# A hybrid decoder step: state copies on the sync queue, sums of the down weights a product ahead, samples without an operand of their own

## The chip, the cores and the metric

The kernel runs on one core of a Trainium2 chip. Its time is device microseconds of one execution; of three runs the median was 1857.97 us (1844.95 to 1858.78). The rows below come from one further, profiled execution, which took 1857.11 us, with a span of 1855.3 us between its first and last recorded instruction.

## The reference, cut to what matters

One decoder layer is computed in float32 for two groups of requests that share the weights: one prompt of 1024 tokens (positions 0 to 1023) and 64 sample tokens (8 requests with 8 tokens each, behind 2048 past tokens).

- RMSNorm, then one input projection (1024 to 1952 columns) that feeds two kinds of attention, a multi-head latent one and a dilated sliding-window one, 8 heads each.
- The heads' outputs pass an output projection (1024 x 1024) and are added to the input: h.
- RMSNorm, then a gated MLP: `g = xn @ w_gate`, `u = xn @ w_up` (1024 x 2816), a causal depthwise convolution of width 3 over g, `silu(gc) * u`, and `@ w_down` (2816 x 1024), added to h. A last RMSNorm gives y.
- Outputs besides y: keys, values and latents of the new tokens, the last rows of g, and **the window state of the samples**: for k and v each, `concatenate([state, new])[-2048:]` along 2048 rows of 512 numbers for 8 requests. 2040 of the 2048 rows are a plain copy from the input, shifted by 8: about 67 MB for k and v together.

## The kernel before, in words

Three phases follow each other, each a block in which the five engines run their own instruction lists, tied by semaphores: `project`, `attention` (the longest) and `output_and_mlp`. Every float32 product is made of three float32r products: a factor is split in a high part (a cast, ACT) and a low part (a subtraction, on DVE or POOL), and high x high, high x low, low x high are added up in PSUM.

**The state copy** (`move`, L192 to L198) is done in 20 chunks of 102 rows. A chunk is four DMAs from DRAM to DRAM, k and v, even and odd rows, 816 KB each. All 80 are issued from ACT's queue: 5 chunks in `project` at the end of a token tile's work (L595), 3 in the output projection (L2724), 12 in the MLP loop after `gate_first(f)` (L2767), f in `moving`. All other DMAs of these phases are issued by SP, in the order in which they are written.

**`project`.** 9 token tiles of 128 rows. For tile t TensorE (PE) makes four groups of projection products (L816), and in between turns the normalised latent `cn` (L828). `cn` comes from PE's first group by way of ACT (squares, L523 and L525), POOL (root) and DVE (L680). SP's list for a tile is `stores(t)`.

**`output_and_mlp`.** The output projection also goes by token tiles (L3102), each followed by a turning of the normalised tile (L3114) whose result ACT and DVE copy and split (`turned`). SP stores h (`store_h`) and loads the next operand (`load_o`).

The MLP is one level of Strassen's scheme in Winograd's form: 7 products of half size for 8. The loop goes over f, 22 blocks of 128 hidden columns (FC = 22). For each f there are 7 products of 24 matmuls (L3122). The weights of block f + 2 are loaded (`load_raw`) as soon as block f's are split; ACT makes high parts, POOL sums and low parts; DVE gathers the results. `gated(f)` makes `us` (the product with silu) and `diff`, the difference of its two token halves (L2897), which lies in the first half of `u3`. `store_a(f)` writes both to scratch `s_a`. `fourth(f)`, which overwrites `u3`, therefore waits for the landing of `diff`'s store (L2907), `up_second(f)` for that of `us` (L2914).

**The down projection** comes last: again 7 products, in the order p1, p2, p5, p3, p6, p7, p4, and each of them in 11 steps (HF = 11) over the hidden dimension, 77 steps n in all. A step is 12 matmuls (L3214): 4 token tiles x 3 float32r terms. The operand from the activations is a piece of `s_a` that SP loads into a ring of 6 places (`load_piece`); for p5, p3 and p6 it is a sum of two pieces, which DVE adds (L2951). The weights `w_down` (11 loads of 1 MB, `load_w`) stay in SBUF; p5, p6, p7 and p4 need differences of their blocks, which POOL makes in place, each right before the step that uses it (L2550). Per step ACT casts both operands (L2671, L2682), DVE makes the low part of the activations (L2840) and POOL that of the weights (L2552). There are 4 operand slots, so these engines can be at most about three steps ahead of PE. When a product is done, DVE adds its four banks to `acc` (L2971); the first add waits for h, which SP has loaded back (`h_in`).

The samples' rows have no halves to combine. In p1, p2, p5 and p3 a step has two more matmuls (L3205) with the samples' activations. For p5 they need a weight block that the product itself doesn't use; it is cast and split into an operand of its own, `extra` (`high_x` L2684, `low_x` L2955).

## Time and profile before

| | us |
|---|---|
| median of 3 runs | 1857.97 |
| lowest, highest | 1844.95, 1858.78 |
| the profiled execution | 1857.11 |
| its span | 1855.3 |

| engine | busy us | share |
|---|---|---|
| PE | 1659.6 | 89% |
| DVE | 1060.3 | 57% |
| ACT | 783.3 | 42% |
| POOL | 961.0 | 52% |

The project phase ends about 290 us into the span, the attention phase at about 902 us, the output projection's first MLP product starts at 1028 us, the MLP loop's second block at 1068 us, and the down projection at 1549 us. In the rows, a line number such as L198 is that of the kernel; "idle before <- releaser" in brackets is how long an engine stood still before an instruction and what ended that; ACTq and SPq are the sequencers of ACT and SP, on which the issue of a DMA takes time.

### The profile page before, as it was taken

What the parts mean: (1) busy time and instruction counts of PE and PEld (TensorE: products, weight loads), DVE (VectorE), ACT (ScalarE), POOL (GpSimd) and SP (SyncE); (2) the same over time, 40 slices, a digit from 0 to 9 for tenths busy, and PEclk for the clock granted to TensorE, in tenths of its full rate; (3) what the DMA queues carried; (4) which work ended last, traced back from release to release, by engine and by line L of the source; (5) the groups of instructions that cost most, each with busy time, mean ns of one, the idle gap of its engine ahead of it and who ended that gap; (6) DMA issues with size and microseconds to landing.
All of it is one profiled execution on the core that took longest, in us unless ns stands there. A gap on an engine that the chain in (4) does not pass through costs nothing.

```text
span 1855.3 us, 29370 instructions
## 1 busy us (share of the span) xinstructions
PE 1659.6 (89%) x10253; PEld 1474.2 (79%) x10253; DVE 1060.3 (57%) x1896; ACT 783.3 (42%) x1639; POOL 961.0 (52%) x825
## 2 busy tenths in 40 slices
PE   7987996999997899999999699899998998979876
PEld 6776775888886788888777699899998997767655
DVE  6523334767775677667443855565554544477664
ACT  5212113666776667666422433333332323333333
POOL 1000001655753668677401877676776762364886
PEclk9998997999999999999999799999999999999999
DMA  8255455233214565655656145546554569634431
GB/s 278 99 170 180 161 175 143 54 101 95 53 52 119 158 175 161 182 160 180 219 152 225 62 126 158 178 159 207 158 156 159 163 207 350 203 108 148 136 115 61
DMA packets 214956, 285.09 MB, mean 154 GB/s; under 512 B 35639, under 2 KB 134584, under 8 KB 209656
## 3 DMA queue, kind: packets, MB, share of 16 engines
q1 hardware_dynamic: 181534, 216.42, 38.2%
q10 hardware_dynamic: 33280, 66.85, 11.0%
q8 instruction: 81, 1.33, 0.3%
q14 instruction: 61, 0.50, 0.1%
HBM read 235.66 MB, written 114.41 MB: 189 GB/s over the span
## 4 chain that ended last, share of the span: by engine, by line
PE 17%; POOL 7%; DMA 6%; DVE 6%; ACTq 6%; issue 4%; ACT 4%; SPq 1%; POOLq 0%; DVEq 0%
ACTq L198 6%; PE r_ps L3122 5%; PE z_ps L3122 3%; POOL d_w L2550 3%; PE q_ps L3122 3%; DMA scratch_s_a<-acc 2%; DMA o_work<-scratch_s_o 2%; POOL lead L2552 1%; POOL u_op L2552 1%; PE q_ps L3102 1%; DMA d_w<-in_w_down 1%; PE v_ps L3122 1%; PE r_ps L3214 1%; PE z_ps L3214 1%; DVE d_ring L2951 1%
## 5 line engine op out<-in xcount | busy, mean ns | idle before, releaser
L1111 POOL TENSOR_SCALAR a_pr<-a_pr,a_rden 128x256 f32<-128x256 f32 (+7 forms) x128 | 94.1, 746 | 192.6 <-DVE a_rden L1211 187.9
L2466 POOL TENSOR_TENSOR lead<-acc,lead 128x512 fp32r<-128x512 f32 x110 | 155.8, 1433 | 38.0 <-ACT lead L2613 37.8
L2840 DVE TENSOR_TENSOR lead<-d_ring,lead 128x512 fp32r<-128x512 f32 x73 | 70.9, 973 | 94.1 <-ACT lead L2671 93.8
L816 PE MATMUL zp<-win_h,xT_h 128*128 128x512 f32 (+1 forms) x288 | 116.4, 404 | 3.3 <-DVE acc L667 3.3
L816 PE MATMUL zp<-win_l,xT_h 128*128 128x512 f32 (+1 forms) x288 | 114.5, 397 | 0.0
L2466 POOL TENSOR_TENSOR u_op<-acc,u_op 128x512 fp32r<-128x512 f32 x44 | 56.6, 1289 | 107.7 <-ACT u_op L2613 98.8
L1152 ACT ACTIVATE a_pr<-a_pr,a_nm 128x256 f32<-128x256 f32 (+7 forms) x128 | 98.5, 772 | 20.0 <-DVE a_nm L1205 19.3
L816 PE MATMUL zp<-win_h,xT_l 128*128 128x512 f32 (+1 forms) x256 | 101.8, 398 | 0.0
L467 POOL TENSOR_TENSOR st<-st 128x2 f32<-128x2 f32 x9 | 1.7, 193 | 189.5 <-ACT cn L525 189.5
L1285 PE MATMUL a_o<-a_ph,a_vh 128*128 128x256 f32 x288 | 87.7, 305 | 13.5 <-DVE a_pl L1215 13.3
L2613 ACT CAST lead<-acc 128x512 fp32r<-128x512 f32 x105 | 62.7, 618 | 74.1 <-PE z_ps L3122 31.1
L2671 ACT CAST lead<-d_ring 128x512 fp32r<-128x512 f32 x73 | 45.1, 618 | 108.4 <-DVE d_ring L2951 52.1
L2552 POOL TENSOR_TENSOR u_op<-d_w,u_op 128x512 fp32r<-128x512 f32 x39 | 53.2, 1366 | 70.0 <-ACT u_op L2682 70.0
L1285 PE MATMUL a_o<-a_pl,a_vh 128*128 128x256 f32 x288 | 82.7, 287 | 0.0
L1285 PE MATMUL a_o<-a_ph,a_vl 128*128 128x256 f32 x288 | 82.5, 286 | 0.0
L3122 PE MATMUL z_ps<-u_s4h,lead 128*128 128x272 f32 x352 | 68.2, 309 | 15.6 <-DVE u_us L2915 15.6
L2552 POOL TENSOR_TENSOR lead<-d_w,lead 128x512 fp32r<-128x512 f32 x38 | 52.2, 1374 | 56.6 <-ACT lead L2682 56.6
L3122 PE MATMUL r_ps<-u_a12h,u_op 128*128 128x272 f32 x352 | 64.1, 295 | 14.0 <-ACT acc L2630 14.0
L1953 ACT CAST w_kth<-l_bank 128x384 fp32r<-128x384 f32 (+2 forms) x96 | 49.5, 517 | 63.5 <-PE l_bank L2051 41.5
L2613 ACT CAST u_op<-acc 128x512 fp32r<-128x512 f32 x42 | 26.0, 621 | 116.3 <-issue 81.3
L1974 DVE TENSOR_TENSOR w_ktl<-l_bank,w_kth 128x384 fp32r<-128x384 f32 (+2 forms) x96 | 57.7, 601 | 27.6 <-ACT w_kth L1953 27.0
L2550 POOL TENSOR_TENSOR d_w<-d_w 128x512 f32<-128x512 f32 x44 | 72.5, 1648 | 0.0
(438 smaller groups left out, 5551.2 us busy)
## 6 DMA issues: line engine op xcount, KB each, us to landing
out_s_win_k<-in_state_win_k ACTq DMA_DIRECT2D x40, 816.0 KB
out_s_win_v<-in_state_win_v ACTq DMA_DIRECT2D x40, 816.0 KB
d_ring<-scratch_s_a SPq DMA_DIRECT2D x106, 256.0 KB, 2.7
acc<-in_state_win_k SPq DMA_DIRECT2D x16, 768.0 KB, 5.6
acc<-in_state_win_v SPq DMA_DIRECT2D x16, 768.0 KB, 5.5
scratch_s_a<-u_us SPq DMA_DIRECT2D x22, 544.0 KB, 6.5
acc<-in_w_gate SPq DMA_DIRECT2D x23, 512.0 KB, 6.5
acc<-in_w_up SPq DMA_DIRECT2D x22, 512.0 KB, 7.4
```

What stands on the lines that cost most here:

```text
L198: eng.dma_start(b[s], a[s]).then_inc(io["moved"], 16)
L816: last = nc.tensor.matmul(z[:, 0:n], a, b, start=(k == 0 and i == 0), stop=(k == KC - 1 and i == len(terms) - 1))
L1111: nc.gpsimd.tensor_scalar(p, p, self.rden[:, k % 2, h:h + 1], 1.0, ALU.mult, ALU.mult)\
L1152: nc.scalar.activation(p, p, ACT.Exp, bias=self.nm[:, k % 2, last, h:h + 1], scale=-1.0, accum_out=self.den[:, k % 2, h:h + 1]).then_inc(S ...
L1285: last = nc.tensor.matmul(self.o_bank[:], x[:, kb, :], y[:, kb], start=(kb == 0 and i == 0), stop=(kb == s and i == 2))
L1974: sub = lambda out, a, b: nc.vector.tensor_tensor(out, a, b.bitcast(F32), ALU.subtract)
L2466: nc.gpsimd.tensor_tensor(op[n][:, 1, :], src, op[n][:, 0, :].bitcast(F32), ALU.subtract).then_inc(S["lo"], 1)
L2550: nc.gpsimd.tensor_tensor(w, a, c, ALU.subtract).then_inc(S["t_sum"], 1)
L2552: nc.gpsimd.tensor_tensor(ob[n % SLOTS][:, 1, :], w, ob[n % SLOTS][:, 0, :].bitcast(F32), ALU.subtract)\
L2613: copy(op[n][:, 0, :], src).then_inc(S["hi"], 1)
L2840: less = lambda out, a, b: tt(out, a, b.bitcast(F32), ALU.subtract)
L3122: last = nc.tensor.matmul(region[:, c * 512:c * 512 + PIECE], op[w][:, a, k * P:(k + 1) * P], X[x][b][:, k, c * PIECE:(c + 1) * PIECE], st ...
```

## The change

1. **State copies.** `move` becomes `move_rows(eng, io, chunk, part)`, one DMA of the four. All 80 are issued by SP: in `project` four in each of the `stores(t)` for t = 2 to 6, one behind the store of the latents, one behind that of the keys, one behind the rotation load and one at the end; in the output projection one behind `load_o` for t < 8; in the MLP loop 2 or 3 at the end of SP's list for each f < 20. ACT issues none.
2. **`diff`.** It gets a place of its own in two halves of 256 columns, made by two subtractions and stored by two DMAs. `fourth(f)` no longer waits for its store; `gated(f)` waits for that of block f - 1.
3. **Order of SP's loads before the down projection.** Pieces 4 to 11 come after six of the eleven weight loads instead of after ten; the other five weight loads are spread over what follows; the ring has 10 places instead of 6.
4. **Sums of the down weights.** p5's differences are made by POOL in p2's steps, p6's by POOL in p3's; p7's and p4's by DVE, two steps ahead.
5. **Samples.** `extra` goes. The samples' sums are taken out of the bank after p1 (into columns 512 to 1023), after p2 (0 to 511, p1 and p2 together) and after p3 (512 to 1023, p5 and p3), so that p5 can use the operand of the product itself. In a product's first step they come last instead of first.

```diff
-def move(eng, io, first, rows):
-
-    for src, dst in (("state_win_k", "s_win_k"), ("state_win_v", "s_win_v")):
...
+def move_rows(eng, io, chunk, part):
+
+    src, dst = (("state_win_k", "s_win_k"), ("state_win_v", "s_win_v"))[part // 2]
+    a = io[src][:, bass.ds(chunk * CHUNK + DEC_T, CHUNK), :].rearrange("b (r s) c -> s b r c", s=2)
+    b = io[dst][:, bass.ds(chunk * CHUNK, CHUNK), :].rearrange("b (r s) c -> s b r c", s=2)
+    eng.dma_start(b[part % 2], a[part % 2]).then_inc(io["moved"], 16)
...
                 store_c(t)
+                move_rows(sp, io, t.n - 2, 0)
                 store_dq(t)
                 store_dk(t)
+                move_rows(sp, io, t.n - 2, 1)
                 store_q(t)
                 if not ends(t):
                     turns_in(t)
+                move_rows(sp, io, t.n - 2, 2)
                 store_dv(t)
                 store_kv(t)
+                move_rows(sp, io, t.n - 2, 3)
...
-                if not isinstance(t.n, int) or t.n == 6:
-                    move(act, io, (t.n - 2) * CHUNK, CHUNK)
...
+        diff0 = ctx.enter_context(nc.sbuf_tensor("u_diff0", [P, 256], F32, side="right"))
...
-        diff = u3[:, 0:512]
+        diff_at = sx_at + DEC_B * (DEC_T + CONV_W - 1)
+        diff = (diff0[:], flat[:, diff_at:diff_at + 256])
...
-                sp.dma_start(s_a[f, :, TOK:A_COLS], diff).then_inc(S["d_st"], 16)
+                for i in range(2):
+                    sp.dma_start(s_a[f, :, TOK + 256 * i:TOK + 256 * i + 256], diff[i]).then_inc(S["d_st"], 16)
...
-                if m >= 10:
-                    sp.wait_ge(S["a_lo"], step_of[m - 6] + 1)
+                if m >= 14:
+                    sp.wait_ge(S["a_lo"], step_of[m - 10] + 1)
...
+                if t < PT:
+                    move_rows(sp, io, 5 + t // 4, t % 4)
...
                 if f:
                     store_a(f - 1)
-            for q, free in ((0, "p1"), (1, "p1"), (2, "p6"), (3, "p6"), (4, "p2"), (5, "p2"), (6, "p7"), (7, "p7"),
-                            (8, "p5"), (9, "p5"), (10, "p4")):
-                sp.wait_ge(S["product"], MADE[free, FC - 1])
-                if q == 10:
-                    for m in range(4, 8):
-                        load_piece(m)
+                for u in range(28 + 52 * f // 20, 28 + 52 * (f + 1) // 20 if f < 20 else 0):
+                    move_rows(sp, io, u // 4, u % 4)
+            made = lambda n: sp.wait_ge(S["product"], MADE[n, FC - 1])
+            for q, n in ((0, "p1"), (1, "p1"), (2, "p6"), (3, "p6"), (4, "p2"), (5, "p2")):
+                made(n)
                 load_w(q)
+            made("p4")
+            for m in range(4, 8):
+                load_piece(m)
+            made("p3")
+            for m in range(8, 12):
+                load_piece(m)
             store_a(FC - 1)
+            load_w(6)
             sp.wait_ge(S["a_st"], 16 * FC)
...
+            load_w(7)
+            sp.wait_ge(S["lo"], 7 * FC)
+            load_h(2, 4)
+            sp.wait_ge(S["a_lo"], 4)
+            load_h(0, 2)
+            load_w(8)
             sp.wait_ge(S["last_ev"], 6)
             sp.dma_start(io["p_ffn_conv"], last_rows[0:CONV_W - 1, :]).then_inc(S["rows_out"], 16)
             sp.dma_start(io["s_ffn_conv"], last_rows[CONV_W - 1:LASTS, :]).then_inc(S["rows_out"], 16)
...
+            load_piece(14)
+            load_w(9)
             sp.wait_ge(S["rows_out"], 32)
             load_h(4, PT)
+            load_piece(15)
+            load_w(10)
+            sp.dma_start(g_last, io["g_final"].partition_broadcast(P)).then_inc(S["h_in"], 16)
...
-                if p in ("p5", "p6", "p7", "p4"):
+                if p == "p2":
                     pool.wait_ge(*w_in(j))
+                    nc.gpsimd.tensor_tensor(w_half(j, 0), w_half(j, 1), w_half(j, 0), ALU.subtract).then_inc(S["t_sum"], 1)
+                elif p == "p3":
                     pool.wait_ge(*w_in(j + HF))
...
+                    pool.wait_ge(S["t_sum"], j + 1)
+                    nc.gpsimd.tensor_tensor(w_half(j, 0), w_half(j + HF, 1), w_half(j, 0), ALU.subtract).then_inc(S["t_sum"], 1)
                 pool.wait_ge(S["b_hi"], n + 1)
...
-            def high_x(j):
...
-                if t % 2 == 0:
-                    move(act, io, (t // 2 + 4) * CHUNK, CHUNK)
...
-                if f in moving:
-                    move(act, io, (8 + moving.index(f)) * CHUNK, CHUNK)
...
-                if n == 5:
+                if n == 4:
                     lasts_out(0, 3)
...
-                tt(diff, us[:, 0:512], us[:, 512:SEQ], ALU.subtract).then_inc(S["act"], 1)
+                if f:
+                    dve.wait_ge(S["d_st"], 32 * f)
+                for i in range(2):
+                    c = 256 * i
+                    last = tt(diff[i], us[:, c:c + 256], us[:, 512 + c:768 + c], ALU.subtract)
+                    last.then_inc(S["act"] if i else S["sink"], 1)
...
                 dve.wait_ge(S["product"], MADE["p7", f])
-                if f:
-                    dve.wait_ge(S["d_st"], 16 * f)
...
-            def low_x(j):
...
+            def third(j):
+                dve.wait_ge(S["t_sum"], HF + j + 1)
+                a = w_half(j, 1)
+                tt(a, w_half(j + HF, 1), a, ALU.subtract).then_inc(S["d_sum"], 1)
+
+            def fourth_sum(j):
+                dve.wait_ge(S["t_sum"], HF + j + 1)
+                dve.wait_ge(S["b_lo"], HF + j + 1)
+                a = w_half(j + HF, 0)
+                tt(a, a, w_half(j, 0), ALU.subtract).then_inc(S["d_sum"], 1)
...
+                if n + 2 < len(STEPS):
+                    p, j = STEPS[n + 2]
+                    if p == "p7":
+                        third(j)
+                    elif p == "p4":
+                        fourth_sum(j)
                 low_a(n)
...
-                if n == 13:
+                if n == 12:
                     dve.wait_ge(S["h_in"], 80)
+                if n in (12, 23, 45):
+                    sample_add(n // HF - 1)
...
                     if k == 3:
+                        if j == 0 and p in ("p1", "p2", "p5", "p3"):
+                            if p in ("p2", "p5"):
+                                pe.wait_ge(S["s_done"], 1 if p == "p2" else 2)
+                            last = sample(p, j, b)
                         last.then_inc(S["step"], 1)
```

## Rows read from the trace of the kernel before

**Rows 1.** The page's top, and its chain of waits by line (shares of the span).
```profile
span 1855.3 us, 29370 instructions
...
ACTq L198 6%; PE r_ps L3122 5%; PE z_ps L3122 3%; POOL d_w L2550 3%; PE q_ps L3122 3%; DMA scratch_s_a<-acc 2%; DMA o_work<-scratch_s_o 2%; POOL lead L2552 1%; POOL u_op L2552 1%; PE q_ps L3102 1%; DMA d_w<-in_w_down 1%; PE v_ps L3122 1%; PE r_ps L3214 1%; PE z_ps L3214 1%; DVE d_ring L2951 1%
```
**Rows 2.** The page's DMA queue of ACT: packets, MB, share of 16 engines' span.
```profile
q10 hardware_dynamic: 33280, 66.85, 11.0%
```
**Rows 3.** Line L198, the copies' issue on ACT: ns min/median/max, first and last start.
```profile
L198 ACTq DMA_DIRECT2D out_s_win_v<-in_state_win_v x40: 679/3592/10944, 100.6 to 1515.1; - x40
```
**Rows 4.** ACT in order of time, one tile of project: start us, us, [idle before <-releaser].
```profile
134.29 10.13 ACTq L198 DMA_DIRECT2D out_s_win_v<-in_state_win_v  x2
144.88 1.07 ACT L512 CAST xT_h<-xp 128x512 fp32r<-128x512 f32 x2 [11.57 <-issue]
```
**Rows 5.** PE's line L828, 98 to 250 us: busy, mean ns | idle before <-releaser.
```profile
L828 PE MATMUL cp<-ident_sb,cn 128*128 128x128 f32 x15 | 4.5, 439 | 24.0 <-DVE cn L680 24.0
```
**Rows 6.** Windows in project: length, busy PE, PEld, DVE, ACT, POOL; PEclk, DMA share, GB/s.
```profile
82.70:245.50 162.80, 138.83 (x626) 116.35 (x624) 47.02 (x127) 28.55 (x70) 8.21 (x20) 0.93 0.50 164
245.50:272.50 27.00, 26.99 (x118) 22.57 (x119) 8.94 (x30) 4.85 (x12) 0.89 (x2) 0.94 0.56 175
```
**Rows 7.** PE in order of time, output projection: the three long stops.
```profile
968.32 0.74 PE L3102 MATMUL z_ps<-lead,o_th 128*128 128x512 f32 x2 [2.79 <-DVE o_tl L2840]
...
997.27 1.54 PE L3114 MATMUL v_ps<-ident_sb,o_work 128*128 128x128 f32 x6 [4.04 <-DVE o_work L2869]
...
1026.57 1.75 PE L3114 MATMUL v_ps<-ident_sb,o_work 128*128 128x128 f32 x7 [6.08 <-DVE o_work L2869]
```
**Rows 8.** Windows of the MLP loop: blocks 1 to 21, block 7, block 15.
```profile
1067.80:1549.10 481.30, 455.45 (x3529) 450.72 (x3529) 267.80 (x276) 161.93 (x336) 326.93 (x227) 0.98 0.54 174
1204.96:1226.11 21.15, 21.15 (x171) 21.14 (x170) 12.65 (x13) 7.56 (x16) 14.50 (x11) 1.00 0.52 169
1381.68:1413.54 31.86, 23.74 (x170) 23.19 (x169) 15.97 (x17) 9.74 (x23) 20.81 (x15) 0.89 0.63 206
```
**Rows 9.** Who waited for whom: us in total, times, longest us.
```profile
DVE acc L2908 <- DMA scratch_s_a<-acc: 52.9, 10, 11.0
```
**Rows 10.** SP's queue in order of time, two blocks of the MLP: start us, us.
```profile
1211.58 0.34 SPq L2343 DMA_DIRECT2D scratch_s_a<-u_us  x1
...
1276.59 3.24 SPq L2343 DMA_DIRECT2D scratch_s_a<-u_us  x1
```
**Rows 11.** The page's DMA issues: KB each, median us from issue to landing.
```profile
scratch_s_a<-u_us SPq DMA_DIRECT2D x22, 544.0 KB, 6.5
```
**Rows 12.** Windows of the down projection: p1 with p2, then p5, p3, p6, p7, p4.
```profile
1549.10:1638.70 89.60, 78.25 (x332) 62.11 (x330) 43.05 (x54) 30.11 (x56) 38.03 (x26) 0.94 0.68 236
1638.70:1687.40 48.70, 39.14 (x154) 29.33 (x155) 36.73 (x38) 17.78 (x32) 25.96 (x18) 0.97 0.36 110
1687.40:1723.00 35.60, 35.60 (x156) 28.97 (x155) 25.41 (x30) 12.87 (x22) 18.41 (x14) 1.00 0.52 161
1723.00:1757.90 34.90, 31.61 (x133) 24.32 (x132) 24.16 (x23) 11.57 (x19) 28.31 (x20) 1.00 0.48 143
1757.90:1803.30 45.40, 33.97 (x132) 25.36 (x132) 30.38 (x29) 17.76 (x32) 36.97 (x33) 0.96 0.38 116
1803.30:1845.10 41.80, 33.06 (x130) 25.17 (x131) 18.66 (x24) 13.92 (x29) 32.07 (x24) 0.96 0.10 26
```
**Rows 13.** The chain of waits in order of time, before DVE's first adds: start us, us.
```profile
1589.99 8.35 DMA acc<-scratch_s_h
```
**Rows 14.** Groups from 1560 us on: POOL's sums and low parts; busy us, mean ns.
```profile
L2550 POOL TENSOR_TENSOR d_w<-d_w 128x512 f32<-128x512 f32 x44 | 72.5, 1648 | 0.0
...
L2552 POOL TENSOR_TENSOR lead<-d_w,lead 128x512 fp32r<-128x512 f32 x36 | 49.1, 1367 | 52.9 <-ACT lead L2682 52.9
```
**Rows 15.** DVE in order of time, two steps of p3.
```profile
1698.80 1.79 DVE L2951 TENSOR_TENSOR d_ring<-d_ring 128x512 f32<-128x512 f32 x1
1701.33 0.69 DVE L2840 TENSOR_TENSOR lead<-d_ring,lead 128x512 fp32r<-128x512 f32 x1 [0.74 <-ACT lead L2671]
```

More of the change, by code:

```diff
@@ L3133, in lasts_turn, with sample @@
                     last.then_inc(S["last_ps"], 1)
+            def sample(p, j, b):
+                rows_s = (sh0 if p in ("p1", "p5") else sh1)[:, j, :]
+                for h in range(2):
+                    last = nc.tensor.matmul(s_bank, rows_s, b[:, h, :], start=p in ("p1", "p5") and j == 0 and h == 0,
+                                            stop=p != "p5" and j == HF - 1 and h == 1, skip_group_check=p == "p2")
+                if p != "p5" and j == HF - 1:
+                    last.then_inc(S["s_ps"], 1)
+                return last
             products(0)
```

97 lines of the change are left out of this document (24 added, 73 removed).

## The prediction

> **What bounds the kernel now.** I start at the page's top and its chain of waits by line. PE is busy for 89% of the span, yet the line with the largest share of the chain is not PE's: it is L198, the issue of the state copies on ACT's queue, with 6% of 1855.3 us, about 110 us [rows 1]. A chain share is an upper bound, not a gain. So the second look goes to each stage: what does PE stand still for, and what ended that wait?
>
> The copies take little DMA time: ACT's queue holds 11.0% of the engines for 80 copies, 204 us / 80 = 2.55 us each [rows 2]. But the issue of one took up to 10.9 us, median 3.6 us for v, which comes third and fourth [rows 3]. In project the last two of a chunk hold ACT for 10.1 us, and its next cast has stood idle for 11.6 us, with nothing but issue before it [rows 4]. That is the whole mechanism: an issuer can run a few copies ahead of the DMA engines, then it stands, and all of ACT's compute stands behind it.
>
> Who waits for ACT there? PE at the turning of the latent: 24.0 us in five tiles [rows 5]. Five tiles with copies last 162.8 / 5 = 32.6 us each; the next one, without, lasts 27.0 us with PE busy throughout [rows 6]. The same three times in the output projection: 2.79, 4.04 and 6.08 us [rows 7]. In the MLP loop a block without disturbance lasts 21.15 us, PE 100% busy; block 15, with ACT held in it and in block 14, lasts 31.86 us, at a granted clock of 0.89, that is partly at 1.2 instead of 2.4 GHz after PE had stood; the 21 blocks last 481.3 us [rows 8]. Part of that stop is not ACT's: `fourth` waits ten times, 52.9 us in all, for the store of `diff` [rows 9].
>
> The down projection is a different case. p3 lasts 35.6 us with PE busy throughout, 3.24 us per step of 14 matmuls; 12 of them are 3.24 x 12/14 = 2.77 us, 30.5 us for 11 steps. p5 lasts 48.7, p7 45.4 and p4 41.8 us [rows 12]. In p7 POOL is busy 36.97 us, in p4 32.07: sum (1.65 us), ACT's cast, low part (1.37 us), one behind the other in every step [rows 14]. Here POOL is the bound. In p5 DVE is, with three instructions per step and 36.73 us busy [rows 12].
>
> **The change part by part.** Gains and losses in us of the profiled execution (1857.1, within 1 of the median of the runs).
>
> *Copies in project.* Five tiles go from 32.6 to 27.0 us: 5 x 5.6 = 28 [rows 6]. ACT's list gets shorter; SP's gets four issues per tile, 4 x 2.55 = 10.2 us of DMA in a tile whose DMA share is 0.50 of 32.6 = 16.3 us, those copies included [rows 2, 6]. 16.3 of 27.0 us fits. Next late would be a store or the next x behind a copy, about 2.6 us; I take 26, bounds 12 and 29.
>
> *Copies in the output projection.* Stops of 12.9 us [rows 7], and clock behind them; eight copies instead of twelve. The first stop came from a late `load_o`, and now a copy follows every `load_o` on the same queue, so part comes back. Bounds 4 and 17; I take 12, because two of the three stops hang on ACT.
>
> *Copies and `diff` in the MLP loop.* 481.3 - 21 x 21.15 = 37 us above the undisturbed block [rows 8]. ACT's hold goes for certain; the wait of `fourth` goes with the new place of `diff` [rows 9]. New: 2.6 copies per block on SP, 6.6 us, behind the weight loads and the stores of their block. DMA is busy 0.54 x 22.9 = 12.4 us per block, copies included [rows 8], so it drains before the next loads. SP's next duty is a block away. The store of `us` already waits 3.24 us for its issue when it follows the weight loads closely, and 0.34 us when it doesn't [rows 10]: SP feels the same limit, but with slack. That store lands 6.5 us after its issue [rows 11]; its user, `up_second`, comes behind the fifth product of the block, and the row with 0.34 us is of block 7, which starts at 1204.96: 1204.96 + 5 x 3.02 (a seventh of 21.15) = 1220.1, 8.5 us after 1211.6 [rows 8, 10]. 2 us of slack. The two subtractions of 256 for one of 512 cost DVE between 0 and 0.7 us (another such instruction, rows 15), covered while DVE is busy 12.65 of 21.15 us [rows 8]; the extra store is one SP issue of 0.34 us. I take 34, bounds 15 and 38.
>
> *Down projection, p1 and p2*: 89.6 us, against 71.2 at 3.24 per step [rows 12]. Earlier pieces take away a stop of PE in p1. But DVE's first adds need all of h, the last of which lands at 1589.99 + 8.35 = 1598.3 [rows 13], 49 us into a stage where the same bytes must still come, and now five weight loads stand among them. Most of p1's gain is therefore waited away again at p2's first step; the sample's wait at p5's first step, now last in it, goes. I take 81, bounds 75 and 92.
>
> *p5*: no `extra` (11 casts, 11 DVE splits), no POOL sum. 35.6 plus 1.4 for bank waits at its start: 37, bounds 35.6 and 42.
> *p3*: POOL gets the sums of p6: two instructions, 3.0 us of 3.24 [rows 14], but no longer with a cast between them. 36.5, bounds 35.6 and 41.
> *p6*: POOL is relieved, and DVE's own cycle of sum, ACT's cast and low part shows: 2.53 us between the starts of rows 15 and 0.6 until the next sum, 3.15 per step against PE's 2.77. The three steps of lead pay for most of the 4 us. 33, bounds 30.5 and 37.
> *p7*: POOL is relieved (36.97 us busy before), DVE gets 11 more sums to its 30.38 us [rows 12]: 11 x 0.7 = 7.5, less the waits for POOL contained in those 30. 37, bounds 31 and 45.
> *p4*: DVE 18.66 + 7 = 26 of 30.5 us. 32.5, bounds 30.5 and 41.8.
> Sum 81 + 37 + 36.5 + 33 + 37 + 32.5 = 257 for 296: 39.
>
> In all 26 + 12 + 34 + 39 = 111: 1857.1 - 111 = **1746 us**.
>
> One row bears on the two engines that share p3, p7 and p4: a DVE sum of two SBUF tiles takes 1.79 us when it starts beside POOL's low part, where the next DVE instruction takes 0.69 [rows 15]. The Trainium skill, page "SBUF — State Buffer", section "Who interferes with whom", has the rule: a DVE instruction with two SBUF inputs and a POOL instruction that reads SBUF exclude each other, for the whole instruction. By that rule the trace agrees, and moving sums from POOL to DVE frees less than it seems.
>
> **Rivals.**
> *DVE and POOL block each other (0.15).* For it: 1.79 against 0.69 us [rows 15], and 11 more such DVE instructions each in p7 and p4. Then p7 and p4 stay at 45.4 and 41.8 and p3 rises to 41 (two POOL instructions of 1.37 and one DVE sum squeezed in, 3.7 per step): 8.4 + 9.3 + 4.5 = 22 less, 1768. Against it: in all three the cast is no longer between two POOL instructions, and both engines can work ahead.
> *Half of the copies' gain comes back (0.12).* SP is held as ACT was [rows 10], and loads and stores behind copies come 2.6 us late each: half of 26 + 12 + 34 is lost, 1782. For it: the 2 us of slack above; against it: DMA share 0.54.
> *Slower (0.02).* Copies of the block before stand in front of `us`'s store in each block: 2.6 x 2.55 = 6.6 us, 20 blocks of 27.8 us, 133 above the floor for 37 now, nothing gained in project and the output projection: 1857 + 96 - 39 = 1914. It decides from the point where DMA work per block passes 21 us; the rows show 12.4. The Trainium skill, page "DMA: Bandwidth & Descriptors", section "Queues, rings and completion order", speaks for this one: DMA engines take turns between queues, but work one queue's descriptors off in order, so a copy on SP's own queue stands wholly in front of what SP issues next. No row here shows that order, as no copy shared SP's queue.
> *No gain (0.03).* ACT's holds were covered and another wait replaces each, as in the chain after a stop; only p5 improves, by 12: 1845. Against it: tile and blocks without copies in rows 6 and 8.
>
> **How the numbers follow.** The forecast has 0.68. For the range: all upper bounds together give 29 + 17 + 38 + 58 = 142, which won't all come; three quarters of the way from 111 is 24, to 1722. Upwards it takes in both middling rivals: 1788. About 1% of the time, 18 us, is what a measurement of this kernel can tell from no change. Faster by over 1%: 0.68 + 0.15 + 0.12 = 0.95, same 0.03, slower 0.02.
>
> **What would show it.** ACT has no DMA issue; no stop of PE at L828 in tiles 2 to 6, tiles of 27 us; every MLP block at 21.2; no wait of L2908's kind for a store; SP's copy issues of up to some us, with nobody waiting. PE's wait at p2's first step for adds after h. p5 at 37, p7 and p4 without POOL as releaser. The forecast is wrong if MLP blocks show DVE waiting for the store of `us`, or if p7 and p4 keep their length with DVE as releaser.

## The result and the profile after

The changed kernel takes 1758.3 us (median of four runs, 1754.4 to 1762.8), the kernel before 1851.5 us (1840.5 to 1858.8): ratio 0.950, 95% interval 0.944 to 0.957. The forecast was 1746 us, range 1722 to 1788. Below, the profiled execution of 1761.3 us, span 1759.5 us.

The windows of the changed kernel that answer to [rows 6, 8, 12]: project's five tiles with copies, the 21 MLP blocks, one of these blocks, then p1 with p2, p5, p3, p6, p7, p4. Columns as there.

```profile
82.80:214.59 131.79, 129.90 (x627) 110.29 (x625) 48.19 (x130) 28.60 (x70) 8.41 (x20) 1.00 0.66 211
1023.25:1489.60 466.35, 447.10 (x3529) 442.76 (x3529) 292.99 (x298) 164.28 (x339) 321.13 (x227) 1.00 0.59 184
1222.54:1244.84 22.30, 21.30 (x171) 21.08 (x170) 13.96 (x14) 7.71 (x17) 15.65 (x11) 1.00 0.63 191
1489.60:1575.90 86.30, 75.68 (x329) 61.01 (x328) 37.87 (x53) 27.94 (x50) 41.66 (x32) 0.92 0.72 250
1575.90:1611.30 35.40, 35.40 (x155) 28.94 (x154) 27.23 (x28) 12.56 (x22) 18.11 (x14) 1.00 0.49 150
1611.30:1647.40 36.10, 36.10 (x158) 29.48 (x157) 28.20 (x28) 11.80 (x21) 30.15 (x20) 1.00 0.49 153
1647.40:1682.90 35.50, 32.71 (x134) 24.13 (x134) 28.49 (x30) 14.16 (x26) 15.83 (x12) 1.00 0.51 155
1682.90:1718.40 35.50, 31.75 (x133) 24.24 (x131) 35.50 (x43) 17.96 (x32) 28.61 (x21) 1.00 0.42 131
1718.40:1748.50 30.10, 29.98 (x130) 24.35 (x130) 24.51 (x29) 12.11 (x25) 23.06 (x15) 1.00 0.09 29
```

The span laid side by side, in us; the cuts are PE's stop ahead of attention, its stop ahead of the output projection, and the first product of MLP block 1:

| stretch | before | after | change | forecast |
|---|---|---|---|---|
| start to attention | 279.05 | 246.55 | -32.5 | -26 |
| attention | 621.4 | 623.2 | +1.8 | 0 |
| output projection and block 0 | 167.4 | 153.5 | -13.8 | -12 |
| MLP blocks 1 to 21 | 481.3 | 466.4 | **-15.0** | **-34** |
| p1 and p2 | 89.6 | 86.3 | -3.3 | -8.6 |
| p5, p3 | 84.3 | 71.5 | -12.8 | -10.8 |
| p6, p7, p4 | 122.1 | 101.1 | -21.0 | -19.6 |
| rest | 10.2 | 11.0 | +0.8 | 0 |
| sum | 1855.3 | 1759.5 | -95.8 | -111 |

The parts of the change were not all taken apart: the down projection's 37 us come from the changed load order, sums and samples together, and the windows show where that gain falls, not which of the three makes it.

One line is far off: the MLP loop. Its clock is 1.00 now and no block is held up by a copy; yet each lasts about 22.3 us instead of 21.15. Two lines of PE's list of waits (total, times, longest); the first heads it and is new:

```profile
PE q_ps L3128 <- DVE acc L2898: 23.1, 20, 4.0
...
PE r_ps L3219 <- DVE acc L2972: 10.6, 1, 10.6
```

L2898 is the add of `second`. It reads PE's bank q_ps, which p7, the fourth product of a block in PE's order, then overwrites. What DVE does ahead of it, from its timeline in one block:

```profile
1228.59 1.29 DVE L2886 TENSOR_TENSOR u_us<-u_us,u_gc 128x1088 f32<-128x1088 f32 x1 [0.55 <-ACT u_gc L2660]
1229.91 1.40 DVE L2892 TENSOR_TENSOR u_diff<-u_us 128x256 f32<-128x256 f32 x1
1231.24 1.51 DVE L2892 TENSOR_TENSOR acc<-u_us 128x256 f32<-128x256 f32 x1
1232.68 0.71 DVE L2898 TENSOR_TENSOR acc<-q_ps,acc 128x544 f32<-128x544 f32 x1
```

and POOL and PE at the same time:

```profile
1228.65 2.38 POOL L2490 TENSOR_TENSOR acc<-acc 128x512 f32<-128x512 f32 x1
1230.99 1.47 POOL L2492 TENSOR_TENSOR acc<-acc 128x512 f32<-128x512 f32 x1
...
1233.44 0.39 PE L3128 MATMUL q_ps<-u_s3h,lead 128*128 128x272 f32 x1 [1.00 <-DVE acc L2898]
```

Two subtractions of 256 columns take 2.9 us; the one of 512 in the kernel before took 1.67. DVE's first ends at 1231.31, just behind POOL's end at 1231.03; its second at 1232.75, behind POOL's end at 1232.46. DVE's instructions end when POOL's do, so cutting one in two bought a second turn of waiting. The same trace holds the counter-example. After the last block POOL does nothing from 1492.07 to 1497.02, and there the same two subtractions take 0.43 and 0.42 us (DVE, then POOL):

```profile
1494.82 0.43 DVE L2892 TENSOR_TENSOR u_diff<-u_us 128x256 f32<-128x256 f32 x1
1495.16 0.42 DVE L2892 TENSOR_TENSOR acc<-u_us 128x256 f32<-128x256 f32 x1
...
1497.02 1.28 POOL L2554 TENSOR_TENSOR u_op<-d_w,u_op 128x512 fp32r<-128x512 f32 x1 [4.96 <-ACT u_op L2686]
```

20 blocks x 1.15 us are 23 us; the time missed the forecast by 12.

The copies of v themselves, now on SP's queue (count, shortest/median/longest issue in ns; those of k are alike), against up to 10.9 us in [rows 3]:

```profile
L197 SPq DMA_DIRECT2D out_s_win_v<-in_state_win_v x40: 674/702/2412, 95.0 to 1436.1; - x40
```

I had expected copy issues "of up to some us" on SP. The longest is 2.5 us and the median 0.7. What follows a copy on SP's queue does feel it: in project the issue of the next x takes 3.2 to 5.2 us in three tiles (below). The short issues made me doubt the reason that I had given for the copies' gain, and half of the experiments are about it.

### The profile page after: what moved, and what is told of

The parts are those of the page before. It is cut to its first block, busy times and chain, and to the rows that moved or that the text cites. A ratio compares the mean times of both kernels' runs of the same rounds, so it can differ in the third digit from the quotient of the medians.

```text
span 1759.5 us, 29359 instructions
## 1 busy us (share of the span) xinstructions
PE 1629.3 (93%) x10253; PEld 1456.8 (83%) x10253; DVE 1092.2 (62%) x1931; ACT 778.7 (44%) x1628; POOL 930.6 (53%) x803
## 4 chain that ended last, share of the span: by engine, by line
PE 21%; DVE 15%; issue 6%; ACT 3%; DMA 3%; POOL 2%; SPq 1%; ACTq 0%; POOLq 0%; DVEq 0%
PE q_ps L3128 4%; PE z_ps L3128 4%; PE v_ps L3128 4%; PE z_ps L3108 3%; DVE d_ring L2945 2%; PE q_ps L3108 2%; DVE acc L2892 2%; PE z_ps L3219 2%; DVE u_gc L2937 1%; DVE u_us L2886 1%; DVE u_gc L2934 1%; ACT u_gc L2660 1%; DVE acc L2972 1%; ACT lead L2673 1%; PE v_ps L3219 1%
## 5 line engine op out<-in xcount | busy, mean ns | idle before, releaser
L2476 POOL TENSOR_TENSOR lead<-acc,lead 128x512 fp32r<-128x512 f32 x110 | 143.7, 1316 | 126.4 <-ACT lead L2615 126.4
L1153 ACT ACTIVATE a_pr<-a_pr,a_nm 128x256 f32<-128x256 f32 (+7 forms) x128 | 98.6, 772 | 22.1 <-DVE a_nm L1206 21.3
L2831 DVE TENSOR_TENSOR lead<-d_ring,lead 128x512 fp32r<-128x512 f32 x73 | 59.0, 808 | 55.0 <-ACT lead L2673 55.0
L2554 POOL TENSOR_TENSOR lead<-d_w,lead 128x512 fp32r<-128x512 f32 x38 | 61.4, 1618 | 54.9 <-ACT lead L2686 54.4
L3128 PE MATMUL q_ps<-u_s3h,lead 128*128 128x272 f32 x352 | 65.3, 298 | 23.2 <-DVE acc L2898 23.1
L2554 POOL TENSOR_TENSOR u_op<-d_w,u_op 128x512 fp32r<-128x512 f32 x39 | 58.2, 1495 | 53.6 <-ACT u_op L2686 53.0
L3128 PEld LDWEIGHTS q_ps<-u_s3h,lead 128*128 128x128 f32 x352 | 51.7, 192 | 27.8 <-DVE acc L2898 27.8
L1286 PEld LDWEIGHTS a_o<-a_ph,a_vh 128*128 128x128 f32 x288 | 56.6, 196 | 18.3 <-issue 15.9
L3128 PE MATMUL z_ps<-u_s4h,lead 128*128 128x272 f32 x352 | 64.0, 295 | 3.1 <-DVE u_us L2909 3.1
L3128 PE MATMUL v_ps<-u_a22h,lead 128*128 128x272 f32 x352 | 64.0, 295 | 1.5 <-issue 1.5
L817 PEld LDWEIGHTS zp<-win_h,xT_h 128*128 128x128 f32 x288 | 54.8, 190 | 12.4 <-DVE acc L668 3.5
```

Source lines behind the costliest of these rows:

```text
L817: last = nc.tensor.matmul(z[:, 0:n], a, b, start=(k == 0 and i == 0), stop=(k == KC - 1 and i == len(terms) - 1))
L1153: nc.scalar.activation(p, p, ACT.Exp, bias=self.nm[:, k % 2, last, h:h + 1], scale=-1.0, accum_out=self.den[:, k % 2, h:h + 1]).then_inc(S ...
L1286: last = nc.tensor.matmul(self.o_bank[:], x[:, kb, :], y[:, kb], start=(kb == 0 and i == 0), stop=(kb == s and i == 2))
L2476: nc.gpsimd.tensor_tensor(op[n][:, 1, :], src, op[n][:, 0, :].bitcast(F32), ALU.subtract).then_inc(S["lo"], 1)
L2554: nc.gpsimd.tensor_tensor(ob[n % SLOTS][:, 1, :], w, ob[n % SLOTS][:, 0, :].bitcast(F32), ALU.subtract)\
L2831: less = lambda out, a, b: tt(out, a, b.bitcast(F32), ALU.subtract)
```

## The experiments

All times are medians; ratios are to the kernel before, with 95% intervals. Each edit is made to the changed kernel unless it says otherwise.

### The copies' part alone: before_sp

The kernel before with nothing changed but `move`: ACT's calls go, and SP gets the calls of `move_rows` at the changed kernel's places.

```diff
-                if f in moving:
-                    move(act, io, (8 + moving.index(f)) * CHUNK, CHUNK)
...
+                for u in range(28 + 52 * f // 20, 28 + 52 * (f + 1) // 20 if f < 20 else 0):
+                    move_rows(sp, io, u // 4, u % 4)
```

> The kernel before, with one part of the change alone: the state copies leave ACT's queue and go on the sync engine's queue, one quarter of a chunk at a time at the changed kernel's places (project, output projection, MLP loop). Difference, down projection and load order as before. Theory A (ACT's hold is the whole cost of the copies and is not paid elsewhere): project -32 us, output projection -14 (both as measured between the two kernels), MLP loop at 21.0 to 21.3 us per block where it was 22.9 on average, -33 or more, the down projection as before; in all 1852 - 80 = 1770 to 1778. Theory B (the difference's new place is needed for the MLP loop's gain, the add's wait for its store stays): MLP blocks 22 or more, 1790 or more. Theory C (only half of the gain, copies in front of stores on the same queue): 1810.

Measured 1772.7 us, 0.958 (0.953 to 0.964): 79 us from the copies. Nineteen MLP blocks and the PE time in them:

```profile
1041.34:1443.34 402.00, 402.00 (x3195) 401.84 (x3193) 243.11 (x248) 146.94 (x304) 298.26 (x210) 1.00 0.62 191
```

402.0 / 19 = 21.16 us per block, PE never idle, with `diff` still in `u3` and its 512 columns in one. So theory A, and the loop's whole gain, about 37 us, was to be had from the copies alone. My terms for the copies (26 + 12 + 34 = 72) were nearly right in sum; the change gave 22 us of them back by another part.

### Engine or group: act_parts, sp_fours, act_fours

Two properties of the copies changed together, the issuing engine and the size of the group. These three kernels fill in the square. "Quarters" means one copy at a time in project and in the output projection, and two or three in a row once per MLP block.

act_parts, quarters on ACT's queue:

```diff
                 gate_first(f)
+                for u in range(28 + 52 * (f - 1) // 20, 28 + 52 * f // 20 if f < 21 else 0):
+                    move_rows(act, io, u // 4, u % 4)
```

> The changed kernel with the state copies back on ACT's queue, but one quarter of a chunk at a time, spread over the tile or over the blocks as they are on the sync engine's queue in the changed kernel (2 or 3 per MLP block). Theory A (the issuing engine is held because it compute-serves PE: any queue hold on ACT costs, and a copy's issue takes ACT 0.7 us and more): ACT is held 0.7 us for each of 80 copies and sometimes longer; in MLP blocks ACT has slack, in project PE waits a little; 1765 to 1800. Theory B (it was the four issues one behind the other that held ACT; apart, each is short, and ACT is as good a place as SP): 1755 to 1764, the same as the changed kernel. Theory C (even a single copy's issue holds ACT for several us): 1820 or more.

sp_fours, four at a time on SP's queue:

```diff
-                move_rows(sp, io, t.n - 2, 0)
...
                 store_kv(t)
+                for i in range(4):
+                    move_rows(sp, io, t.n - 2, i)
```

> The changed kernel with the state copies on the sync engine's queue, but four at a time, where and as often as ACT issued them in the kernel before (at the end of a tile of project, three times in the output projection, after 12 of the MLP blocks' loads and stores). Theory A (which engine issues decides; SP has nobody behind it that is urgent): 1755 to 1768, as the changed kernel, although the third and fourth issue of a group takes SP 3 to 8 us. Theory B (the small parts decide: 3.3 MB in one go stand in front of weight loads and stores on the same queue, 10 us of DMA): a store of us or a load of the next x comes late, PE stands some us per group of 20, 1790 to 1830.

act_fours, four at a time on ACT's queue, as in the kernel before:

> The changed kernel with the state copies on ACT's queue again and four at a time, as and where the kernel before has them. It completes a square: on SP in quarters 1758 us, on ACT in quarters 1763, on SP in fours 1832. Theory A (the engine is nothing, the group of four is the whole cost): 1825 to 1840. Theory B (ACT's own queue keeps the copies from standing in front of loads and stores on SP's queue, but they hold ACT): between, 1852 less 37 for the down projection, 1805 to 1820.

| | quarters, spread | four at once |
|---|---|---|
| on SP | 1758.3, 0.950 (0.944 to 0.957) | 1831.6, 0.988 (0.983 to 0.994) |
| on ACT | 1763.2, 0.952 (0.947 to 0.958) | 1835.2, 0.990 (0.988 to 0.993) |

Down a column the intervals overlap; along a row it is 73 and 72 us. **The group is the cost; the engine makes no difference that these times can tell.** Four in a row also means fewer places further apart, and no run separates the two. The issues on ACT in quarters, then on SP in fours, then on ACT in fours (v alone for ACT; those of k are short, as on SP):

```profile
L197 ACTq DMA_DIRECT2D out_s_win_v<-in_state_win_v x40: 679/680/2331, 91.9 to 1454.3; - x40
```

```profile
L197 SPq DMA_DIRECT2D out_s_win_k<-in_state_win_k x40: 675/697/1076, 100.9 to 1519.4; - x40
L197 SPq DMA_DIRECT2D out_s_win_v<-in_state_win_v x40: 706/3532/8359, 103.0 to 1522.1; - x40
```

```profile
L197 ACTq DMA_DIRECT2D out_s_win_v<-in_state_win_v x40: 679/3801/12268, 102.4 to 1525.1; - x40
```

The third and fourth of a group (v) hold their engine for a median of 3.5 to 3.8 us on either; in quarters they don't. What the hold hits is different. On SP it hits the next load. SP's timeline at the end of the first tile of project with copies, in sp_fours:

```profile
100.94 1.91 SPq L197 DMA_DIRECT2D out_s_win_k<-in_state_win_k  x2
103.02 9.53 SPq L197 DMA_DIRECT2D out_s_win_v<-in_state_win_v  x2
112.87 5.04 SPq L295 DMA_DIRECT2D acc<-in_x_prompt  x1
```

then ACT's and PE's in the same kernel:

```profile
128.88 1.06 ACT L503 ACTIVATE acc<-acc 128x1024 f32<-128x1024 f32 x1 [17.98 <-DMA acc<-in_x_prompt]
...
133.55 0.80 PE L793 MATMUL cp<-wkv_h,cT_h 128*128 128x512 f32 x1 [9.93 <-DVE qm L666]
```

The next x is issued 12 us late and is there 16 us after that. ACT and DVE work their lists in order and have x ahead of `qm`, for which PE's next product waits, so PE stands 9.93 us. On ACT, in act_fours, the hold hits the next cast, as in [rows 4], and PE stands 5.93 us in the same tile:

```profile
102.36 10.38 ACTq L197 DMA_DIRECT2D out_s_win_v<-in_state_win_v  x2
112.92 1.07 ACT L511 CAST xT_h<-xp 128x512 fp32r<-128x512 f32 x2 [12.20 <-issue]
```

The rule that I cited for the slower rival (a queue's transfers are worked off in order, the Trainium skill, page "DMA: Bandwidth & Descriptors", section "Queues, rings and completion order") is in line with this load of x behind the copies. The time from its issue alone doesn't prove order, as a full set of DMA engines would delay it too, but the four kernels speak against that. From issue to landing the three loads of x that follow copies take 14.9 to 15.8 us in sp_fours and 8.6 to 10.7 in act_fours, where as many copies are under way on the other queue. With the copies spread it is 14.4 to 18.1 us in the changed kernel and 8.4 to 8.9 in act_parts. Their issue, in the changed kernel and in act_parts:

```profile
L295 SPq DMA_DIRECT2D acc<-in_x_prompt x3: 3203/3550/5163, 101.4 to 154.9; - x3
L295 SPq DMA_DIRECT2D acc<-in_x_prompt x3: 349/355/358, 100.7 to 152.6; - x3
```

So the queue is not nothing: what stands behind a copy on the copy's own queue comes about 6 us later, even with spread copies. Here that was nearly covered. ACT waited up to 9.94 us for x in the changed kernel, and PE stood once, for 1.90 us.

For act_parts theory B held, for sp_fours theory B, for act_fours theory A. My own theory A for sp_fours, that SP has nobody urgent behind it, fell.

### The late add: late_diff, diff_back, copy_diff, psum_diff

late_diff moves the two subtractions behind the add:

```diff
                 gated(f - 1)
                 second(f)
+                differ(f - 1)
```

> The changed kernel, with the two subtractions of 256 columns moved on DVE behind the add of the fourth up-product's half (the second form on u2), which PE's product q_ps<-u_s3h waits for. In the changed kernel every MLP block lasts 22.30 us with 1.00 us of PE standing before that product, released by this add; DVE does two subtractions of 1.40 and 1.51 us in front of it, where the kernel before had one of 1.67. Theory A (the two subtractions on DVE's path to that add are the whole stop): blocks of 21.15 to 21.3 us, 21 x 1.1 = 23 us less than the changed kernel's 1758, so 1735. Theory B (DVE is late anyway, by the add's place in a cycle that the sigmoid unit and DVE set, ACT's silu to the tap sums): the stop moves to the next product, blocks 22.0 or more, 1752 to 1760.

1733.8 us, 0.937 (0.933 to 0.941). DVE in one block, and then the window of 19 blocks:

```profile
1229.05 1.29 DVE L2886 TENSOR_TENSOR u_us<-u_us,u_gc 128x1088 f32<-128x1088 f32 x1 [0.55 <-ACT u_gc L2660]
1230.26 0.71 DVE L2900 TENSOR_TENSOR acc<-q_ps,acc 128x544 f32<-128x544 f32 x1
1230.89 0.88 DVE L2894 TENSOR_TENSOR u_diff<-u_us 128x256 f32<-128x256 f32 x1
1231.69 1.51 DVE L2894 TENSOR_TENSOR acc<-u_us 128x256 f32<-128x256 f32 x1
```

```profile
1034.52:1433.92 399.40, 399.40 (x3194) 399.40 (x3193) 254.02 (x267) 146.28 (x304) 296.52 (x210) 1.00 0.63 192
```

21.02 us per block, PE without a gap. Theory A: the same instructions in another order, still beside POOL (0.88 and 1.51 us), but with nobody waiting for them; 24 us.

diff_back undoes part 2 of the change and keeps the rest:

```diff
-        diff = (diff0[:], flat[:, diff_at:diff_at + 256])
+        diff = u3[:, 0:512]
...
                 dve.wait_ge(S["product"], MADE["p7", f])
+                if f:
+                    dve.wait_ge(S["d_st"], 16 * f)
```

> The changed kernel with one part undone: the difference is again one subtraction of 512 columns into the tile u3 with one store, and the add that overwrites u3 waits for that store; the state copies stay on the sync engine's queue in small parts. Theory A (in the kernel before, the wait for that store was a consequence of ACT's held copies and full queues; with the copies spread it is short): PE's stop before q_ps<-u_s3h is gone since DVE does one subtraction of 1.67 us; the store is issued at +1.6 us and lands 4 us later, about when the add wants to start, so blocks of 21.2 to 21.6 us, 1735 to 1745 us in all. Theory B (the new place of the difference was needed): the add waits for the store in most blocks by 2 us or more, and blocks are 22.3 or longer, 1758 or more.

1736.4 us, 0.938 (0.934 to 0.942), blocks of 401.75 / 19 = 21.14 us. `fourth` still waits for the store:

```profile
L2898 DVE TENSOR_TENSOR acc<-q_ps,acc 128x544 f32<-128x544 f32 x20 | 14.5, 724 | 31.0 <-DMA scratch_s_a<-acc 24.4 <-PE q_ps L3124 6.6
```

24.4 us in all over 20 blocks, and PE is busy 401.62 of 401.75 us: the wait fits into slack. before_sp, which keeps it, has no stop of PE in its 19 blocks either. What the wait of 52.9 us in [rows 9] cost PE, with groups of copies in the way, isn't separated; a hint is that PE's stops behind the add of `up_second`, which DVE does next, come to 15.6 us in the kernel before and to 4.4 us in act_fours, which has the groups and not the wait. With the copies spread the new place for `diff` bought nothing, and being in two halves `diff` cost 22 us.

copy_diff puts a plain copy in the place of each subtraction, which leaves out the difference:

```diff
-                    last = tt(diff[i], us[:, c:c + 256], us[:, 512 + c:768 + c], ALU.subtract)
+                    last = nc.vector.tensor_copy(diff[i], us[:, c:c + 256])
```

> The changed kernel, with each of the two subtractions of 256 columns replaced by a plain copy of the first operand (leaves out the difference itself, so the scratch holds other values). Same places, sizes, waits and stores. Theory A (the 1.40 and 1.51 us of a 256-column subtraction are not its own work but its turn against POOL's instruction of 1.3 to 2.4 us that runs beside it, since both read two SBUF tiles): with one SBUF input the copy takes under 0.5 us, PE's stop of 1.00 us goes, blocks 21.15 to 21.3, time about 1735. Theory B (a 256-column instruction on DVE costs that much by its size): the copies take 1.2 us or more each and the blocks stay at 22.3, 1758.

It came out as theory B had it: 1755.6 us, 0.949 (0.943 to 0.954), PE's stop still 0.75 us, and DVE's groups (mean ns after the busy time) hardly shorter:

```profile
L2892 DVE COPY acc<-u_us 128x256 f32<-128x256 f32 x19 | 26.2, 1380 | 0.0
L2892 DVE COPY u_diff<-u_us 128x256 f32<-128x256 f32 x19 | 24.0, 1266 | 0.6
```

So "two SBUF inputs" doesn't draw the line. But the experiment did not tell the theories apart as I had set it up: the Trainium skill, page "SBUF — State Buffer", section "Who interferes with whom", says that a copy too may take the interface that DVE shares with POOL. An instruction of the same size that has one input in PSUM should not. That is psum_diff, which also leaves out the difference:

```diff
+                        last = tt(diff[i], Q[:, 0:256], us[:, c:c + 256], ALU.subtract)
```

> The changed kernel, with the first operand of each of the two subtractions of 256 columns taken from PE's result q_ps in PSUM instead of from us (leaves out the difference itself, so the scratch holds other values); size, place, output tiles and stores unchanged. A plain copy from SBUF in that place took 1.27 and 1.38 us, hardly less than the subtraction's 1.40 and 1.51, so the number of SBUF inputs did not tell the two theories apart. Theory A (DVE waits for POOL's running instruction to end whenever it wants the SBUF interface that both share, and a plain copy of SBUF to SBUF wants it too): the adds that read PSUM and one SBUF tile take 0.71 us for 544 columns beside the same POOL work, so these take 0.35 to 0.45 us, PE's stop of 1.00 us goes and the blocks last 21.0 to 21.2 us, 1735 us. Theory B (an instruction of 256 columns is slow at this place for another reason, such as its outputs or a start-up of its own): 1.2 us or more each, 1758.

1733.2 us, 0.936 (0.932 to 0.940):

```profile
L2894 DVE TENSOR_TENSOR u_diff<-q_ps,u_us 128x256 f32<-128x256 f32 x19 | 8.1, 424 | 1.3 <-PE q_ps L3132 0.7
```

0.42 us for the same columns at the same place beside the same POOL work. The instruction's own time is 0.4; the other 1.0 us was the wait for POOL. The kernels show the same without any edit: the tap sum of 64 columns, and the subtraction of 512, in diff_back (shortest/median/longest ns):

```profile
L2887 DVE TENSOR_TENSOR acc<-u_us x20: 691/1662/1679, 1047.0 to 1447.7; 128x512 f32<-128x512 f32 x20
L2930 DVE SCALAR_TENSOR_TENSOR u_gc<-acc,u_coef,u_gc x20: 280/1321/1325, 1061.4 to 1463.1; 128x64 f32<-128x64 f32 x20
```

64 columns take 0.28 us once and 1.32 us otherwise. With that rule of the Trainium skill the trace agrees, for the copy and for the input in PSUM.

### The wait at p2: h_ahead

DVE's first add of the down projection waited 13.75 us, and not for h (SP's queue, then DVE):

```profile
1522.39 0.36 SPq L2368 DMA_DIRECT2D acc<-scratch_s_h  x1
...
1523.82 0.59 SPq L2452 DMA_DIRECT2D d_ring<-in_g_final  x1
```

```profile
1536.49 0.68 DVE L2980 TENSOR_TENSOR acc<-v_ps,acc 64x512 f32<-64x512 f32 x1 [13.75 <-DMA d_ring<-in_g_final]
```

`g_final` counts on h's semaphore and is needed only at the end; the changed order of SP's loads has put it last, behind h and all the weight loads.

```diff
-                    dve.wait_ge(S["h_in"], 80)
+                    dve.wait_ge(S["h_in"], 64)
...
             load_h(4, PT)
+            load_w(8)
             load_piece(15)
+            load_w(9)
```

> The changed kernel, with the gain g_final on a semaphore of its own (DVE's first adds of the down projection wait for the four loads of h alone) and with three weight loads (pieces 8, 9 and 10) behind the load of h's second half instead of among the loads of h. In the changed kernel PE stands 10.6 us at the start of p2, DVE's first add having waited to 1536.49 for the load of g_final, which was the last in the queue; the last load of h was issued at 1522.39 and took about 9 us. Theory A (order of the queue and the shared semaphore are the cause): h is there by about 1528, before PE's stop at 1529.9, the stop goes down to 0 to 2 us, the first step of p2 runs at full clock, and the time falls by 9 to 13 us to 1745 to 1749. Theory B (the bytes in flight are the bound, DMA being at 400 GB/s from 1485 to 1523): what is taken from the stop comes back at p2's weights or pieces, and the gain is under 4 us.

1749.9 us, 0.947 (0.942 to 0.951). That interval overlaps the changed kernel's, but the stage shows it (p1 with p2, then DVE's first add):

```profile
1487.26:1564.00 76.74, 74.74 (x330) 60.24 (x329) 37.99 (x53) 27.80 (x49) 41.90 (x32) 0.98 0.79 281
```

```profile
1525.51 0.68 DVE L2980 TENSOR_TENSOR acc<-v_ps,acc 64x512 f32<-64x512 f32 x1 [5.13 <-DMA acc<-scratch_s_h]
```

76.7 us instead of 86.3, PE's stop 2.0 instead of 10.6 us. Theory A. Which half of the edit did it, the semaphore or the order, wasn't separated; by the times above, 1536.49 less the 1522.39 + 9.3 us in which h's second half landed, the semaphore is worth about 5 of the 10. The whole kernel gained 8.4 us, just under theory A's 9.

Why h's second half is issued only at 1522.39 is a wait that neither the change nor this edit touches. SP first waits for the landing of the two stores of the last rows of g. In the changed kernel (chain of waits: start us, us):

```profile
1507.58 14.79 DMA out_s_ffn_conv<-acc
```

It was 5.19 us in the kernel before and is 12.35 in h_ahead, where h is still the end of DVE's wait. No run moves these stores.

### Who makes the sums: sums_pool

```diff
+                if p == "p5":
...
+                    nc.gpsimd.tensor_tensor(w_half(j, 1), w_half(j + HF, 1), w_half(j, 1), ALU.subtract).then_inc(S["d_sum"], 1)
+                elif p == "p6":
...
+                    nc.gpsimd.tensor_tensor(w_half(j + HF, 0), w_half(j + HF, 0), w_half(j, 0), ALU.subtract).then_inc(S["d_sum"], 1)
...
-                    if p == "p7":
-                        third(j)
-                    elif p == "p4":
-                        fourth_sum(j)
```

> The changed kernel with the block sums of products p7 and p4 on POOL instead of DVE, one product further ahead: p7's sum in p5's steps, p4's in p6's steps, so that POOL does one sum and one low part in each step of p2, p5, p3 and p6 (3.0 us of a step of 2.8 to 3.25) and DVE none. In the changed kernel DVE is busy 35.50 of the 35.5 us of p7 and releases PE with waits of 0.4 to 0.5 us per step. Theory A (DVE's two added sums are p7's bound): p7 goes from 35.5 to 31.5 us, p6 with 1.6 + 1.4 us of POOL per step of 2.8 us grows a little; net -3 to +1, 1755 to 1760. Theory B (POOL and DVE take turns at SBUF, so the sums cost the same wherever they are, and POOL's step is now too long in p5 and p6): p5 and p6 go up by 4 or more each, 1766 to 1775.

1752.2 us, 0.947 (0.942 to 0.952), not to be told from the changed kernel by time. The windows of p6 and p7:

```profile
1641.00:1678.90 37.90, 32.94 (x133) 24.15 (x133) 30.33 (x30) 14.55 (x26) 34.67 (x22) 1.00 0.51 158
1678.90:1709.40 30.50, 30.50 (x134) 24.85 (x133) 29.40 (x30) 17.91 (x32) 26.42 (x23) 1.00 0.51 164
```

p7 35.5 to 30.5, p6 35.5 to 37.9: DVE was p7's bound, and POOL becomes p6's when it has two instructions in a step of 2.8 us. p5, with a step of 3.2 us, takes them without loss (35.42 us, PE busy throughout). So only p7's sum should move, into p5. The five products together took 169.8 for 172.6 us: theory A.

In the changed kernel itself p6's step is set by DVE. A sum beside POOL, ACT's cast and DVE's low part follow each other every 3.14 us, and ACT's second cast and POOL's low part hang on the same round:

```profile
1661.80 1.78 DVE L2945 TENSOR_TENSOR d_ring<-d_ring 128x512 f32<-128x512 f32 x1
1664.32 0.69 DVE L2831 TENSOR_TENSOR lead<-d_ring,lead 128x512 fp32r<-128x512 f32 x1 [0.74 <-ACT lead L2673]
1664.93 1.79 DVE L2945 TENSOR_TENSOR d_ring<-d_ring 128x512 f32<-128x512 f32 x1
```

PE's steps start at the same pace, at 1663.18, 1666.32 and 1669.47.

### Together: late_h and best

late_h is late_diff with h_ahead; best adds p7's sum on POOL in p5's steps, p4's staying on DVE.

> The first two of these edits together, without the third: the difference behind the add on u2, and the loads of h ahead of three weight loads, with g_final on its own semaphore. Theory A (they add): 1758 - 24 - 8.4 = 1726. Theory B (the DMA queues bound p1 and p2 when the loop before them is shorter): 1730 to 1734. Beside the kernel with all three edits it gives the worth of p7's sum on POOL: 5 us if DVE was p7's bound, 0 if POOL's added instruction is paid for in p5.

> Three edits on the changed kernel together: the two subtractions of the difference behind the add on u2 (alone: 1734 us, from 1758), the loads of h ahead of three weight loads with g_final on its own semaphore (alone: 1750), and the block sum of product p7 on POOL in p5's steps instead of on DVE (with p4's sum on POOL as well, p5 to p4 took 170 us for 173; p7 fell from 35.5 to 30.5 us while p6 rose from 35.5 to 37.9). Theory A (three stops at three places of PE, so the gains add up): 24 + 8.4 + 5 (p7 at 31, p6 no longer than 35.5) = 37 less, 1721 us. Theory B (a shorter MLP loop and earlier loads make DMA late in p1 and p2, since the bytes are the same): h is as late as before relative to p2, and the gain is 29 or less, 1729 or more.

late_h 1725.7 us, 0.934 (0.930 to 0.938); **best 1720.2 us, 0.929 (0.926 to 0.931)**, 38 us under the changed kernel. In best p6 and p7 last

```profile
1611.30:1646.40 35.10, 32.73 (x133) 24.12 (x133) 27.26 (x30) 14.55 (x26) 15.81 (x12) 1.00 0.56 170
1646.40:1676.90 30.50, 30.50 (x134) 24.82 (x132) 30.06 (x31) 18.02 (x32) 25.59 (x23) 1.00 0.45 144
```

The gains add up to within a few us, since they are stops at different places of PE: theory A. The third is shown by the windows; the intervals of the two times overlap.

## Why the prediction was right, and where not

- **Sign and size** right: 1758 for 1746, in the range. In part that is luck: project gave 6.5 us more than forecast and the MLP loop 19 less, and the two offset each other.
- **Copies in project**: -32.5 for -26, above my upper bound of 29. The five tiles went from 162.8 to 131.8 us, 26.4 each, where I had taken 27.0 as the floor, from a tile in [rows 6] at a clock of 0.94; at 1.00 the shortest lasted 25.9. I had also allowed 2 us for stores and loads behind a copy, and that came: PE's one stop in the five tiles, 1.90 us, follows from a late x behind a copy. What I had too high was the floor.
- **Copies in the output projection**: -13.8 for -12, right.
- **The mechanism of the copies** was wrong in one half. That "an issuer can run a few copies ahead of the DMA engines, then it stands" is right: with four in a row the third and fourth stand; with one to three at a time the longest issue was 2.6 us. "ACT's hold goes for certain", because the queue is SP's, is not the reason: with ACT as issuer it goes as well, and with SP in groups of four nearly the whole gain of the copies is gone. The rival "half of the copies' gain comes back" describes sp_fours, where 73 us came back; I gave it no condition on the group's size, which is what decides.
- **MLP loop**: -15 for -34, the step that failed. It said that the two subtractions "cost DVE between 0 and 0.7 us", "covered while DVE is busy 12.65 of 21.15 us". Two errors. The price was read from an instruction of DVE with POOL idle; beside POOL it was 1.2 us, which [rows 15] showed and I used only for the down projection. And the cover was a mean over the block: DVE idles elsewhere, while between the silu and `second` it runs without a break, and PE waits right behind. With one subtraction the blocks are at 21.14 and the time is 1736 (diff_back).
- **`diff`'s wait** [rows 9] was counted as part of the stop that the new place would take away. With the copies spread it needs no new place: diff_back has 24.4 us of it, all hidden.
- **p1 and p2**: -3.3 for -8.6. The wait at p2's first step came as forecast, 10.6 us, but I named the last h as its end; about half of it was `g_final` on the same semaphore, and h itself was late behind SP's wait for the stores of the last rows.
- **p5, p3, p7, p4**: 35.4, 36.1, 35.5, 30.1 for 37, 36.5, 37, 32.5: right. p6 35.5 for 33: DVE's cycle came as I had it, 3.14 us per step for 3.15, and 11 such steps are 34.6 us. What failed is "the three steps of lead pay for most of the 4 us": they paid for next to nothing. PE's listed stops there name POOL's low parts (1.7 us) and DVE's adds (0.7), but POOL waits for a cast of ACT, and ACT makes it after another cast, for which it waits for DVE's sum (22.1 us in ten waits).
- **The lock rival** (0.15) placed the lock in p7 and p4. There it cost less than the rival had it: p7 ended up bound by DVE at 35.5, not 45.4. But it was there: p7's eight sums that start in its window take 1.36 us on average, against 0.68 for the shortest, 5.5 us more in all. That is the size of what p7 loses to best's 30.5, though no run shows that the two are the same. I had priced the sums at 0.7. It struck hardest in the MLP loop, where I didn't look for it.
- **Two slips of arithmetic**, without weight: 11 x 0.7 is 7.7, not 7.5, and three quarters of the way from 111 to 142 is 23, not 24.

## What to carry to other kernels

Price an instruction by its neighbours in time, not by its columns: beside POOL a DVE instruction from SBUF to SBUF costs up to the rest of POOL's running one, so two small ones cost more than one large. Ask of a cover where in the period it lies, and put work that nobody waits for behind the add that PE waits for. Spread bulk copies, one to three at a time; which of the two queues they are on made no difference to the time here, but what follows a copy on its own queue came 6 us later, so keep urgent loads off it or early. Look at what else counts on a semaphore before you name the wait.

## What the runs showed of the hardware

- A DMA issue of 816 KB takes a median of 0.68 to 0.70 us on ACT or SP when copies are spread (longest 2.6), and the third and fourth of a group of four up to 12.3 us on ACT and 8.4 us on SP.
- A load of x behind spread copies: 14.4 to 18.1 us from issue to landing on the copies' own queue, 8.4 to 8.9 us with the copies on the other.
- A DVE subtraction of 256 columns beside POOL: 1.40 and 1.51 us with both inputs in SBUF, 1.27 and 1.38 us as a copy, 0.42 us with one input in PSUM; with POOL idle 0.43 and 0.42 us with both inputs in SBUF.
